# Low parts of five up units per turn made by an accumulating GpSimd DMA in the two gate/up stages

## The chip, the cores and the metric

The kernel runs on one core of one Trainium2 chip. The metric is device time of one execution in microseconds (us). The kernel before took 2433.75 us (median of 3 runs, 2433.02 to 2434.05).

## The reference

One decoder layer for 256 tokens of width 2048, in float32. The two feed-forward blocks are what the change touches; the width of each is 5632.

```
x = x + 0.5 * swiglu(rmsnorm(x, g_ffn1), w1_gate, w1_up, w1_down)
... (latent attention, dilated attention, gates, output projection)
x = x + 0.5 * swiglu(rmsnorm(x, g_ffn2), w2_gate, w2_up, w2_down)
... (per-layer embedding gate)
swiglu(h, wg, wu, wd) = (silu(h @ wg) * (h @ wu)) @ wd
```

All weights are float32 in HBM and are read once.

## The kernel before

Every product of float32 matrices is made of three matmuls of type float32r. A weight w is split into a rounded high part `wh` (the write to float32r rounds it) and a low part `wl` = w - `wh`; the activations are split alike. Then x w is taken as xh wh + xh wl + xl wh.

Weights stream in **units** of 128 x 1024 values (512 KB). Unit n uses slot n mod 4 of three rings, `raw`, `wh` and `wl`. Four engines work on it, each in its own fixed order, tied by counting semaphores:

- SP issues the load into `raw` (`square`, line 291) once the unit that used the slot before has its low part (`lo_ready`).
- ACT writes `wh` from `raw` (`split`, line 903, `hi_ready`) once the load has landed and PE is done with unit n-4 (`unit_done` at n-3).
- DVE writes `wl` = `raw` - `wh` (line 1310, `lo_ready`).
- PE waits for `lo_ready` and makes 12 matmuls of 512 columns (lines 444 to 446).

A gate/up stage has 11 **turns** of 512 output columns, with 16 units each, v0 to v15: even units are of the gate matrix, odd ones of the up matrix, and units 2p and 2p+1 are pair p, which covers two blocks of 128 rows. In turns 1 to 9 (`FAST_TURNS`) the pairs 1, 3 and 5 (`FAST_PAIRS`: v2, v3, v6, v7, v10, v11) are made by a scheme of Strassen's kind with 21 matmuls in place of 24 (lines 551 to 553). For it DVE also builds sums of weight blocks (`sums`, lines 1413 to 1416), ACT rounds them (`TH`, line 1000) and DVE takes their low parts (`TL`, line 1421). Before v14, PE turns the finished block of the turn before with 8 transposes (line 454). ACT and DVE work four units ahead: in the loop step of v they split v+4.

Both stages are written out unit by unit. The GpSimd engine (POOL) does nothing after the start.

Of the kernel before, what the change touches and what calls it, by code (L numbers as in the profile page):

```python
# [5 lines left out]
ALU = mybir.AluOpType  # L6
ACT = mybir.ActivationFunctionType
# [7 lines left out]
P = 128  # L15
BANK = 512
SLOTS = 4
# [32 lines left out]
def hybrid_layer(nc, out, x, p, positions, g_ffn1, w1_gate, w1_up, w1_down, g_mix, w_in, g_cq, w_uq,  # L50
# [16 lines left out]
    T, KD, KF = S // P, D // P, FF // P  # L67
# [7 lines left out]
    FFN_TURNS, FFN_BODY = FF // BANK, 2 * KD // 2  # L75
# [6 lines left out]
    UNITS = sum(counts)  # L82
# [3 lines left out]
    with ExitStack() as ctx:  # L86
        def sem(name):
            return ctx.enter_context(nc.semaphore(name))
# [27 lines left out]
        def whole(name, where, shape, dt=F32):  # L116
            return nc.alloc_sbuf_tensor_at(name, shape, dt, offset=front + where)
# [4 lines left out]
        raw = whole("raw", 48 * KB, [P, SLOTS, UNIT])  # L122
        wh = whole("wh", 64 * KB, [P, SLOTS, UNIT], F32R)
        wl = whole("wl", 80 * KB, [P, SLOTS, UNIT], F32R)
# [62 lines left out]
        raw_in = [sem(f"raw_in{j}") for j in range(SLOTS)]  # L187
        hi_ready, lo_ready = sem("hi_ready"), sem("lo_ready")
        unit_done = sem("unit_done")
        x_first, x_in = sem("x_first"), [sem(f"x_in{j}") for j in range(4)]  # L190
        ident_in, row1_in, rows_in, consts_in, gains_in, p_in = (
            sem(n) for n in ("ident_in", "row1_in", "rows_in", "consts_in", "gains_in", "p_in"))
# [38 lines left out]
        FAST_TURNS, FAST_PAIRS = range(1, FFN_TURNS - 1), (1, 3, 5)  # L231


        def fast(n):
            m, v = divmod(n, FFN_BODY)
            return n < FFN_TURNS * FFN_BODY and m in FAST_TURNS and v // 2 in FAST_PAIRS

        TURN_FASTS = len(FAST_TURNS) * len(FAST_PAIRS)
        FASTS = TURN_FASTS + 2 * len(DOWN_PAIRS)

# [8 lines left out]
        def fasts_down(r, half, k):  # L249

            return (r // 2) * FASTS + TURN_FASTS + half * len(DOWN_PAIRS) + DOWN_PAIRS.index(k // 2)

# [27 lines left out]
        def _(sp):  # L280
            def wide(n, j, w, k, c0, width=UNIT, waits=1):

                sp.wait_ge(lo_ready, n + waits - SLOTS)
                sp.dma_start(raw[:, j % SLOTS, 0:width], w[0, k * P:(k + 1) * P, ds(c0, width)])\
                  .then_inc(raw_in[j % SLOTS], 16)

            def square(n, j, w, k, c0, waits=1):

                if waits and not (isinstance(n, int) and n < SLOTS):
                    sp.wait_ge(lo_ready, n + waits - SLOTS)  # L290
                sp.dma_start(raw[:, j % SLOTS, :].rearrange("p (k c) -> p k c", k=2),
                             w[0, k * P:(k + 2) * P, ds(c0, BANK)].rearrange("(k p) c -> p k c", p=P))\
                  .then_inc(raw_in[j % SLOTS], 16)
# [53 lines left out]
            def projection(u0, c0):  # L347
                for k in range(KD):
                    wide(u0 + k, k, w_in, k, c0)
# [5 lines left out]
            for k in range(KD):  # L355
                wide(U_LAT + k, k, w_in, k, 0, LAT)
# [14 lines left out]
            j = 0  # L371
# [4 lines left out]
            with sp.Fori(1, MERGE_TURNS) as i:  # L376
                j = 0
                for w, c0, K in ((w_in, OFF_GATE, KD), (w_br_mla, 0, H), (w_in, OFF_GATE + D, KD), (w_br_dil, 0, H)):
                    for k in range(0, K, 2):


                        waits = 2 if j == KD // 2 - 1 else 0 if j == KD // 2 else 1
# [7 lines left out]
            j = 0  # L390
# [18 lines left out]
        def _(pool):  # L409
            for s in (a_ready, res_ready, dil_turned, dil_T, dil_ready, m_ready, mprod_ready):  # L410
                pool.sem_inc(s, PRIMED)
            pool.memset(ones[:, :], 1.0).then_inc(ones_ready, 1)


        @block.tensor
        def _(pe):
            def wide_tile(j, t, k, hi, lo, b0, width, K):

                s = j % SLOTS
                cols = [(c, min(width, c + BANK)) for c in range(0, width, BANK)]  # L420
                xh, xl = hi[:, k, t * P:(t + 1) * P], lo[:, k, t * P:(t + 1) * P]
                for a, w, first, last in ((xh, wh, k == 0, False), (xh, wl, False, False), (xl, wh, False, k == K - 1)):
                    for m, (c, e) in enumerate(cols):
                        mm = pe.matmul(ps[:, b0 + 2 * t + m, 0:e - c], a, w[:, s, c:e], start=first, stop=last)  # L424
                return mm

            def wide_unit(n, j, k, hi, lo, b0, width, K):

                pe.wait_ge(lo_ready, n + 1)
                for t in range(T):  # L430
                    mm = wide_tile(j, t, k, hi, lo, b0, width, K)
                mm.then_inc(unit_done, 1)

            def square_unit(n, j, k, hi, lo, b0, K):


                pe.wait_ge(lo_ready, n + 1)
                s = j % SLOTS
                for t in range(T):
                    for kk in range(2):  # L440
                        xh, xl = (a[:, k + kk, t * P:(t + 1) * P] for a in (hi, lo))
                        c = slice(kk * BANK, (kk + 1) * BANK)
                        first, last = k + kk == 0, k + kk == K - 1
                        pe.matmul(ps[:, b0 + t, :], xh, wh[:, s, c], start=first, stop=False)  # L444
                        pe.matmul(ps[:, b0 + t, :], xh, wl[:, s, c], start=False, stop=False)  # L445
                        mm = pe.matmul(ps[:, b0 + t, :], xl, wh[:, s, c], start=False, stop=last)  # L446
                mm.then_inc(unit_done, 1)
# [95 lines left out]
            def fast_pair(n, j, p, hi, lo, forms, sum_hi, sum_lo, first, last, b0, c12, c21, b1, count):  # L543

                s, s1, ka, kb = j % SLOTS, (j + 1) % SLOTS, 2 * p, 2 * p + 1

                def product(bank, x, w, start, stop):
                    (xh, xl), (yh, yl) = x, w  # L550
                    pe.matmul(ps[:, bank, :], xh, yh, start=start, stop=False)  # L551
                    pe.matmul(ps[:, bank, :], xh, yl, start=False, stop=False)  # L552
                    return pe.matmul(ps[:, bank, :], xl, yh, start=False, stop=stop)  # L553

                def block(k, t):
                    return hi[:, k, t * P:(t + 1) * P], lo[:, k, t * P:(t + 1) * P]

                def weights(slot, c):
                    return wh[:, slot, c * BANK:(c + 1) * BANK], wl[:, slot, c * BANK:(c + 1) * BANK]

                S1, S3, S2, S4 = forms
                T1, T3, T2, T4 = ((sum_hi[:, a, :], sum_lo[:, a, :]) for a in range(4))
                pe.wait_ge(lo_ready, n + 1)
                product(b0, block(kb, 0), weights(s, 1), False, False)
                product(b1, block(ka, 0), weights(s, 0), first, last).then_inc(unit_done, 1)
                pe.wait_ge(lo_ready, n + 2)
                product(c12, S4, weights(s1, 1), False, False).then_inc(unit_done, 1)
                pe.wait_ge(TL_ready, 2 * count + 1)
                product(b1 + 2, S3, T3, first, last)
                product(b1 + 3, S1, T1, first, last)  # L570
                pe.wait_ge(TL_ready, 2 * count + 2)
                product(b1 + 1, S2, T2, first, last)
                product(c21, block(kb, 1), T4, False, False).then_inc(fast_done, 1)
# [145 lines left out]
            for k in range(KD):  # L719
                if k == 10:  # L720
# [3 lines left out]
                    for a in range(2):  # L724
                        for h2 in range(H // 2):
                            for t in range(T):
                                c0 = (h2 % 2) * S + t * P
# [84 lines left out]
            j = KD  # L812
# [8 lines left out]
            with pe.Fori(1, MERGE_TURNS) as i:  # L821
                j = 0
# [26 lines left out]
            j = 0  # L849
            for h in range(2):  # L850
# [21 lines left out]
                if h == 0:  # L872
                    for k in range(PLE // P):
                        wide_unit(U_PLE + j, j, k, pTh, pTl, 4, UNIT, PLE // P)
                        j += 1
            pe.wait_ge(lo_ready, UNITS)
            for t, c0, c1, b in LAST:
                if b < 4:
                    pe.wait_ge(psig_ready, T + 1)
# [10 lines left out]
        def _(act):  # L890
# [5 lines left out]
            def split(n, j):  # L896

                first = isinstance(n, int) and n < SLOTS
                act.wait_ge(raw_in[j % SLOTS], ((n - j % SLOTS) * (16 // SLOTS) + 16) if not isinstance(n, int)
                            else 16 * (n // SLOTS + 1))  # L900
                if not first:
                    act.wait_ge(unit_done, n - (SLOTS - 1))
                act.activation(wh[:, j % SLOTS, :], raw[:, j % SLOTS, :], ACT.Copy).then_inc(hi_ready, 1)  # L903

            def ahead(n, j):
                split(n + SLOTS, j)
# [249 lines left out]
            for k in range(KD):  # L1156
# [10 lines left out]
                if k in (3, 4, 5, 6):  # L1167
                    if k == 3:
                        act.wait_ge(mla_inv, 1)
                    t, a = (k - 3) // 2, (k - 3) % 2  # L1170
                    for h in range(H):
                        c = (a * T + t) * H + h
                        src, step = ((q_tok, QK), (kv_tok, NOPE + HD))[a]
                        v = src[:, t, h * step:h * step + NOPE]
# [6 lines left out]
                if k in (11, 13):  # L1181
                    for h in range((k - 11) * 2, (k - 11) * 2 + 4, 2):
                        act.wait_ge(mla_turned, 2 + h + 1)
                        for a in range(2):
                            ins = act.activation(nT[:, h, a, :], ps[:, 4 + h % 4, a * S:(a + 1) * S], ACT.Copy,
                                                 scale=gcol[:, 4 * KD + NG + a:4 * KD + NG + a + 1])
# [77 lines left out]
            with act.Fori(0, MERGE_TURNS - 1) as i:  # L1264
                for j in range(MERGE_BODY):
                    n = U_MERGE + MERGE_BODY + i * MERGE_BODY + j
# [14 lines left out]
            j = 0  # L1281
# [22 lines left out]
        def _(dve):  # L1304
            chain = Chain(dve, dve_step)

            def split(n, j):

                dve.wait_ge(hi_ready, n + 1)
                dve.tensor_tensor(wl[:, j % SLOTS, :], raw[:, j % SLOTS, :], wh[:, j % SLOTS, :].bitcast(F32),  # L1310
                                  ALU.subtract).then_inc(lo_ready, 1)
# [362 lines left out]
            for k in range(KD):  # L1674
# [4 lines left out]
                if k < T:  # L1679
                    qr = rh[:, k, 0, :, :]  # L1680
                    q_rot = q_tok[:, k, :].rearrange("p (h c) -> p h c", h=H)[:, :, NOPE:QK]
                    c, s = (b[:, k, 0:half].unsqueeze(1).to_broadcast([P, H, half]) for b in (cos, sin))
# [119 lines left out]
            with dve.Fori(0, MERGE_TURNS - 1) as i:  # L1802
                for j in range(MERGE_BODY):
                    n = U_MERGE + MERGE_BODY + i * MERGE_BODY + j
# [14 lines left out]
            j = 0  # L1819
# [74 lines left out]
```

## Time and profile before

| | before |
|---|---|
| median of 3 runs | 2433.75 us |
| span of the profiled execution | 2432.5 us |
| PE busy, of the span | 2417.7 us, 99% |
| DVE busy | 1765.8 us, 73% |
| ACT busy | 1309.0 us, 54% |
| POOL busy | 0.4 us |
| DMA queue of SP | 455.52 MB, 58.8% of 16 engines |

The only times there are for the kernel as a whole are those of the three runs; the profiled execution has its span, from its first to its last instruction. A busy share is an average over stages. The first gate/up stage runs from the start to about 480 us, the second ends at about 2090 us. The timeline gives the start of an instruction, its length, and in brackets how long its engine sat idle before it and who ended that. A matmul is shown as 0.39 us long but the next starts 0.227 us later, since they overlap.

### The profile page before, as it was taken

The page shows a single profiled execution, that of the slowest core. Times are in us where ns is not written, and L with a number is a line of the kernel's source. Part 1 is how long each engine was busy: PE and PEld are TensorE (multiplying, and loading weights), DVE is VectorE, ACT ScalarE, POOL GpSimd, SP SyncE. Part 2 cuts the span into 40 slices and gives each one's busy share as a digit, 9 for nine tenths or more (in the row PEclk, how much of TensorE's full clock was granted, in tenths as well). Part 3 has the DMA queues.
Part 4 walks back from the last instruction along what each step waited for, and adds up shares of the span by engine and source line. Part 5 has one row for each costly group of instructions (what it writes and reads, how often), then busy time and mean ns, then how long its engine had stood idle before and what let it go on. Part 6 is the DMA issues. An engine that isn't in the chain of part 4 may idle for free.

```text
span 2432.5 us, 29257 instructions
## 1 busy us (share of the span) xinstructions
PE 2417.7 (99%) x11104; PEld 2009.4 (83%) x11104; DVE 1765.8 (73%) x2136; ACT 1309.0 (54%) x1594; POOL 0.4 (0%) x5
## 2 busy tenths in 40 slices
PE   9999999999999999999999999999999999999999
PEld 7888888878888877888888888888888888878887
DVE  6888989688876665657655455558898987787765
ACT  6555555554555665454454444455555555554553
POOL 0000000000000000000000000000000000000000
PEclk9999999999999999999999999999999999999999
DMA  7665656646656654655634666556565666566654
GB/s 241 195 212 182 214 184 207 199 166 214 191 188 193 182 157 132 196 182 181 191 116 127 200 190 191 189 184 201 184 207 183 205 200 201 180 200 200 206 186 165
DMA packets 192237, 457.54 MB, mean 188 GB/s; under 512 B 14632, under 2 KB 16624, under 8 KB 192112
## 3 DMA queue, kind: packets, MB, share of 16 engines
q1 hardware_dynamic: 191664, 455.52, 58.8%
q8 instruction: 80, 1.31, 0.2%
q14 instruction: 45, 0.37, 0.0%
q10 hardware_dynamic: 448, 0.34, 0.0%
HBM read 453.70 MB, written 2.10 MB: 187 GB/s over the span
## 4 chain that ended last, share of the span: by engine, by line
PE 95%; DVE 4%; ACT 1%; issue 0%; DMA 0%; SPq 0%; ACTq 0%
PE ps L424 37%; PE ps L444 13%; PE ps L446 13%; PE ps L445 13%; PE ps L551 5%; PE ps L553 5%; PE ps L552 5%; PE ps L622 1%; PE ps L454 1%; PE ps L638 1%; DVE wl L1310 1%; PE ps L462 1%; ACT wh L903 1%; PE ps L649 0%; DVE aTl L1471 0%
## 5 line engine op out<-in xcount | busy, mean ns | idle before, releaser
L1310 DVE TENSOR_TENSOR wl<-raw,wh 128x1024 fp32r<-128x1024 f32 x786 | 952.2, 1222 | 566.9 <-ACT wh L903 561.3
L903 ACT ACTIVATE wh<-raw 128x1024 fp32r<-128x1024 f32 x786 | 824.1, 1057 | 815.0 <-PE ps L424 400.1
L444 PE MATMUL ps<-wh,hT 128*128 128x512 f32 x1232 | 483.8, 393 | 2.1 <-DVE hT L1330 1.4
L446 PE MATMUL ps<-wh,hT 128*128 128x512 f32 x1232 | 480.1, 390 | 0.0
L445 PE MATMUL ps<-wl,hT 128*128 128x512 f32 x1232 | 480.0, 390 | 0.0
L424 PE MATMUL ps<-wh,hT 128*128 128x512 f32 (+1 forms) x1536 | 415.0, 388 | 1.2 <-DVE om L1576 1.0
L424 PEld LDWEIGHTS ps<-wh,hT 128*128 128x128 f32 x1536 | 283.6, 188 | 57.5 <-issue 1.2
L444 PEld LDWEIGHTS ps<-wh,hT 128*128 128x128 f32 x1232 | 231.8, 188 | 49.8 <-DVE hT L1330 1.7
L446 PEld LDWEIGHTS ps<-wh,hT 128*128 128x128 f32 x1232 | 231.6, 188 | 48.4
L445 PEld LDWEIGHTS ps<-wl,hT 128*128 128x128 f32 x1232 | 231.9, 188 | 46.7
L424 PE MATMUL ps<-wl,hT 128*128 128x512 f32 (+1 forms) x768 | 234.5, 387 | 0.0
L424 PEld LDWEIGHTS ps<-wl,hT 128*128 128x128 f32 x768 | 143.0, 188 | 29.1
L1000 ACT ACTIVATE TH<-sums 128x1024 fp32r<-128x1024 f32 x108 | 114.7, 1062 | 89.1 <-DVE sums L1413 65.9
L424 PE MATMUL ps<-wh,aTh 128*128 128x512 f32 x512 | 158.1, 390 | 0.0
L424 PE MATMUL ps<-wl,aTh 128*128 128x512 f32 x512 | 157.7, 389 | 0.0
L424 PE MATMUL ps<-wh,aTl 128*128 128x512 f32 x512 | 157.6, 389 | 0.0
L1421 DVE TENSOR_TENSOR TL<-sums,TH 128x1024 fp32r<-128x1024 f32 x108 | 127.1, 1218 | 0.0
L424 PEld LDWEIGHTS ps<-wl,aTh 128*128 128x128 f32 x512 | 96.1, 188 | 20.1
L424 PEld LDWEIGHTS ps<-wh,aTl 128*128 128x128 f32 x512 | 96.1, 188 | 20.0
L424 PEld LDWEIGHTS ps<-wh,aTh 128*128 128x128 f32 x512 | 95.7, 188 | 19.9 <-DVE wl L1310 0.2
L993 ACT ACTIVATE wh<-raw 128x512 fp32r<-128x512 f32 x78 | 49.3, 632 | 69.8 <-PE ps L446 30.4
L1000 ACT ACTIVATE TH_d<-sums_d 128x1024 fp32r<-128x1024 f32 x48 | 51.0, 1062 | 33.2 <-DVE sums_d L1413 22.3
(277 smaller groups left out, 2790.2 us busy)
## 6 DMA issues: line engine op xcount, KB each, us to landing
raw<-in_w_in SPq DMA_DIRECT2D x208, 512.0 KB, 3.6
raw<-in_w_gate SPq DMA_DIRECT2D x176, 512.0 KB, 3.7
raw<-in_w_up SPq DMA_DIRECT2D x176, 512.0 KB, 4.5
raw<-in_w_down SPq DMA_DIRECT2D x176, 512.0 KB, 4.4
raw<-in_w_o SPq DMA_DIRECT2D x32, 512.0 KB, 4.0
raw<-in_w_ple_gate SPq DMA_DIRECT2D x32, 512.0 KB, 3.5
raw<-in_w_br_mla SPq DMA_DIRECT2D x16, 512.0 KB, 4.8
raw<-in_w_br_dil SPq DMA_DIRECT2D x16, 512.0 KB, 3.7
```

Of the source, the lines that this page charges most:

```text
L424: mm = pe.matmul(ps[:, b0 + 2 * t + m, 0:e - c], a, w[:, s, c:e], start=first, stop=last)
L444: pe.matmul(ps[:, b0 + t, :], xh, wh[:, s, c], start=first, stop=False)
L445: pe.matmul(ps[:, b0 + t, :], xh, wl[:, s, c], start=False, stop=False)
L446: mm = pe.matmul(ps[:, b0 + t, :], xl, wh[:, s, c], start=False, stop=last)
L551: pe.matmul(ps[:, bank, :], xh, yh, start=start, stop=False)
L552: pe.matmul(ps[:, bank, :], xh, yl, start=False, stop=False)
L553: return pe.matmul(ps[:, bank, :], xl, yh, start=False, stop=stop)
L903: act.activation(wh[:, j % SLOTS, :], raw[:, j % SLOTS, :], ACT.Copy).then_inc(hi_ready, 1)
L993: act.activation(wh[:, s, BANK:UNIT], raw[:, s, BANK:UNIT], ACT.Copy).then_inc(hi_ready, 1)
L1000: act.activation(dst[:, 2 * a:2 * a + 2, :], src[:, 2 * a:2 * a + 2, :], ACT.Copy).then_inc(TH_ready, 1)
L1310: dve.tensor_tensor(wl[:, j % SLOTS, :], raw[:, j % SLOTS, :], wh[:, j % SLOTS, :].bitcast(F32), ALU.subtract).then_inc(lo_ready, 1)
L1421: dve.tensor_tensor(dst[:, 2 * a:2 * a + 2, :], src[:, 2 * a:2 * a + 2, :], hi[:, 2 * a:2 * a + 2, :].bitcast(F32), ALU.subtract).then_inc ...
```

## The change

Five units of each of the turns 1 to 9, v1, v5, v9, v13 and v15 (all of the up matrix, `by_dma`), get their low part in another way. ACT writes `wh` as before, then writes the negated rounded weight into `wl`, and only then counts up `hi_ready`. POOL waits for that and issues a DMA that reads the same 512 KB of weights from HBM once more and adds them to what stands in `wl`. DVE skips these units. PE waits for the DMA (`sum_in`) instead of `lo_ready`. SP frees the `raw` slot of such a unit by `hi_ready`. There are 45 such units in a stage and 90 in all. All counts of `lo_ready` are lowered by the number of such units before (`lows`).

```diff
+        def by_dma(n):
+            if not isinstance(n, int):
+                return False
+            n -= U_GU2 if n >= U_GU2 else U_GU1
+            m, v = divmod(n, FFN_BODY)
+            return m in FAST_TURNS and v % 2 == 1 and v // 2 not in FAST_PAIRS
...
@@ SP
                 if waits and not (isinstance(n, int) and n < SLOTS):
-                    sp.wait_ge(lo_ready, n + waits - SLOTS)
+                    if by_dma(n - SLOTS):
+                        sp.wait_ge(hi_ready, n - SLOTS + 1)
+                    else:
+                        sp.wait_ge(lo_ready, lows(n + waits - SLOTS))
...
@@ POOL
+            def low_parts(u0, w_gate, w_up):
+                for m in FAST_TURNS:
+                    for v in range(FFN_BODY):
+                        n, k, c0 = u0 + m * FFN_BODY + v, v // 2 * 2, m * BANK
+                        if by_dma(n):
+                            pool.wait_ge(hi_ready, n + 1)
+                            pool.dma_start(wl[:, n % SLOTS, :].rearrange("p (k c) -> p k c", k=2),
+                                           (w_gate, w_up)[v % 2][0, k * P:(k + 2) * P, c0:c0 + BANK]
+                                           .rearrange("(k p) c -> p k c", p=P), accum_op=ALU.add)\
+                                .then_inc(sum_in[n % SLOTS // 2], 16)
...
@@ PE, square_unit
-                pe.wait_ge(lo_ready, n + 1)
+                if by_dma(n):
+                    pe.wait_ge(sum_in[n % SLOTS // 2], 16 * sums_in(n))
+                else:
+                    pe.wait_ge(lo_ready, lows(n + 1))
...
@@ ACT, split
-                act.activation(wh[:, j % SLOTS, :], raw[:, j % SLOTS, :], ACT.Copy).then_inc(hi_ready, 1)
+                high = act.activation(wh[:, j % SLOTS, :], raw[:, j % SLOTS, :], ACT.Copy)
+                if by_dma(n):
+                    high = act.activation(wl[:, j % SLOTS, :], raw[:, j % SLOTS, :], ACT.Copy, scale=-1.0)
+                high.then_inc(hi_ready, 1)
...
@@ DVE, split
+                if by_dma(n):
+                    return
```

On ACT, before, from the split of v4 on in turn 2 (the last two rows make the sums of pair 3):

```order
L903 ACTIVATE wh<-raw 128x1024 [waits unit_done,raw_in0]
L903 ACTIVATE wh<-raw 128x1024 [waits unit_done,raw_in1]
L903 ACTIVATE wh<-raw 128x1024 [waits unit_done,raw_in2]
L993 ACTIVATE wh<-raw 128x512 [waits unit_done,raw_in3]
L1000 ACTIVATE TH<-sums 128x1024 [waits fast_done,sums_ready]
L1000 ACTIVATE TH<-sums 128x1024 [waits sums_ready]
```

The same place on ACT in the changed kernel:

```order
L941 ACTIVATE wh<-raw 128x1024 [waits unit_done,raw_in0]
L941 ACTIVATE wh<-raw 128x1024 [waits unit_done,raw_in1]
L943 ACTIVATE wl<-raw 128x1024
L941 ACTIVATE wh<-raw 128x1024 [waits unit_done,raw_in2]
L1034 ACTIVATE wh<-raw 128x512 [waits unit_done,raw_in3]
L1041 ACTIVATE TH<-sums 128x1024 [waits fast_done,sums_ready]
L1041 ACTIVATE TH<-sums 128x1024 [waits sums_ready]
```

One pass over the slot of v5 has come in between its high part and that of v6.

On SP, before, the loads of v4 to v9 of a turn:

```order
L291 DMA raw<-in_w_gate 128x2x512 [waits lo_ready]
L291 DMA raw<-in_w_up 128x2x512 [waits lo_ready]
L291 DMA raw<-in_w_gate 128x2x512 [waits lo_ready]
L291 DMA raw<-in_w_up 128x2x512 [waits lo_ready]
L291 DMA raw<-in_w_gate 128x2x512 [waits lo_ready]
L291 DMA raw<-in_w_up 128x2x512 [waits lo_ready]
```

The same loads in the changed kernel:

```order
L312 DMA raw<-in_w_gate 128x2x512 [waits lo_ready]
L312 DMA raw<-in_w_up 128x2x512 [waits hi_ready]
L312 DMA raw<-in_w_gate 128x2x512 [waits lo_ready]
L312 DMA raw<-in_w_up 128x2x512 [waits lo_ready]
L312 DMA raw<-in_w_gate 128x2x512 [waits lo_ready]
L312 DMA raw<-in_w_up 128x2x512 [waits hi_ready]
```

The order is the same; v5 and v9 now wait for ACT's second pass over v1 and v5 in place of DVE's low part.

On PE, before, the last rows of a unit and the start of v5, the fourth row here:

```order
L444 MATMUL ps<-wh,hT 128x512
L445 MATMUL ps<-wl,hT 128x512
L446 MATMUL ps<-wh,hT 128x512
L444 MATMUL ps<-wh,hT 128x512 [waits lo_ready]
L445 MATMUL ps<-wl,hT 128x512
L446 MATMUL ps<-wh,hT 128x512
```

The same place on PE in the changed kernel:

```order
L482 MATMUL ps<-wh,hT 128x512
L483 MATMUL ps<-wl,hT 128x512
L484 MATMUL ps<-wh,hT 128x512
L482 MATMUL ps<-wh,hT 128x512 [waits sum_in0]
L483 MATMUL ps<-wl,hT 128x512
L484 MATMUL ps<-wh,hT 128x512
```

Nothing moved; the wait ahead of the unit is now for the accumulating DMA. On POOL there are 90 DMAs `wl<-in_w_up`, each waiting for `hi_ready`, and nothing else.

## Rows read from the trace of the kernel before

**Rows 1.** Page, parts 1 and 2: busy us of each engine, and PE's granted clock.

```profile
PE 2417.7 (99%) x11104; PEld 2009.4 (83%) x11104; DVE 1765.8 (73%) x2136; ACT 1309.0 (54%) x1594; POOL 0.4 (0%) x5
...
PEclk9999999999999999999999999999999999999999
```

**Rows 2.** Windows (PE, PEld, DVE, ACT, POOL busy; clock; DMA share; GB/s): turn 2, both down stages.

```profile
100.33:142.70 42.37, 42.37 (x192) 35.18 (x192) 37.48 (x39) 24.14 (x26) 0.00 (x0) 1.00 0.63 199
483.00:700.00 217.00, 214.36 (x941) 176.51 (x940) 178.83 (x218) 116.84 (x127) 0.00 (x0) 0.99 0.59 195
2090.00:2300.00 210.00, 207.64 (x914) 171.55 (x913) 168.34 (x181) 113.19 (x120) 0.00 (x0) 0.99 0.58 192
```

**Rows 3.** Groups by line, 57 to 433 us: busy, mean ns, idle before.

```profile
L444 PE MATMUL ps<-wh,hT 128*128 128x512 f32 x353 | 138.0, 391 | 0.0
...
L903 ACT ACTIVATE wh<-raw 128x1024 fp32r<-128x1024 f32 x115 | 119.4, 1055 | 91.5 <-PE ps L446 48.7 <-DMA raw<-in_w_gate 40.2 <-DMA raw<-in_w_up 1.5
...
L1310 DVE TENSOR_TENSOR wl<-raw,wh 128x1024 fp32r<-128x1024 f32 x116 | 139.5, 1221 | 39.8 <-ACT wh L903 38.7
```

**Rows 4.** Waits of PE, 483 to 700 us: total, times, longest.

```profile
PE ps L551 <- DVE wl L1403: 2.5, 1, 2.5
```

**Rows 5.** Timeline of ACT, turn 2.

```profile
106.18 1.05 ACT L903 ACTIVATE wh<-raw 128x1024 fp32r<-128x1024 f32 x1
...
109.59 1.07 ACT L903 ACTIVATE wh<-raw 128x1024 fp32r<-128x1024 f32 x1 [2.36 <-DMA raw<-in_w_gate]
...
116.28 1.99 ACT L903 ACTIVATE wh<-raw 128x1024 fp32r<-128x1024 f32 x2
119.88 1.06 ACT L903 ACTIVATE wh<-raw 128x1024 fp32r<-128x1024 f32 x1 [1.61 <-DMA raw<-in_w_gate]
...
130.40 1.06 ACT L903 ACTIVATE wh<-raw 128x1024 fp32r<-128x1024 f32 x1 [0.21 <-DMA raw<-in_w_up]
131.37 0.58 ACT L969 ACTIVATE ends<-ps 128x512 f32<-128x512 f32 x1
...
136.68 1.06 ACT L903 ACTIVATE wh<-raw 128x1024 fp32r<-128x1024 f32 x1 [1.66 <-PE ps L446]
```

**Rows 6.** Timeline of PE, turn 2 and the start of turn 3.

```profile
105.82 0.39 PE L551 MATMUL ps<-wh,hT 128*128 128x512 f32 x1
...
113.30 0.39 PE L444 MATMUL ps<-wh,hT 128*128 128x512 f32 x1
...
116.02 0.39 PE L551 MATMUL ps<-wh,hT 128*128 128x512 f32 x1
...
123.50 0.39 PE L444 MATMUL ps<-wh,hT 128*128 128x512 f32 x1
...
133.70 0.39 PE L444 MATMUL ps<-wh,hT 128*128 128x512 f32 x1
...
136.42 1.03 PE L454 MATMUL ps<-ident,gs 128*128 128x128 f32 x8
...
140.03 0.39 PE L444 MATMUL ps<-wh,hT 128*128 128x512 f32 x1
...
145.47 0.39 PE L444 MATMUL ps<-wh,hT 128*128 128x512 f32 x1
```

**Rows 7.** DMA, 57 to 433 us: queue share; issues, KB, median us to landing.

```profile
q1 hardware_dynamic: 38848, 74.89, 62.0%
...
raw<-in_w_gate SPq DMA_DIRECT2D x74, 512.0 KB, 3.8
raw<-in_w_up SPq DMA_DIRECT2D x69, 512.0 KB, 4.6
```

**Rows 8.** Timeline of SP's DMA queue, turn 2: issue and its length.

```profile
105.71 0.37 SPq L291 DMA_DIRECT2D raw<-in_w_gate  x1
106.12 1.69 SPq L291 DMA_DIRECT2D raw<-in_w_up  x1
109.12 0.37 SPq L291 DMA_DIRECT2D raw<-in_w_gate  x1
111.58 0.37 SPq L291 DMA_DIRECT2D raw<-in_w_up  x1
```

More of the change, by code:

```diff
@@ L189, in hybrid_layer @@
         unit_done = sem("unit_done")
+        sum_in = [sem(f"sum_in{a}") for a in range(2)]
         x_first, x_in = sem("x_first"), [sem(f"x_in{j}") for j in range(4)]
@@ L236, in fast, with lows, sums_in @@
             return n < FFN_TURNS * FFN_BODY and m in FAST_TURNS and v // 2 in FAST_PAIRS
+        def by_dma(n):
[4 more added lines that the diff above has]
+            return m in FAST_TURNS and v % 2 == 1 and v // 2 not in FAST_PAIRS
+        def lows(n):
+            return n - (sum(by_dma(i) for i in range(n)) if isinstance(n, int) else TURN_DMAS)
+        def sums_in(n):
+            return sum(by_dma(i) and i % SLOTS == n % SLOTS for i in range(n + 1))
+        TURN_DMAS = len(FAST_TURNS) * (KD // 2 - len(FAST_PAIRS))
         TURN_FASTS = len(FAST_TURNS) * len(FAST_PAIRS)
@@ L289, in square @@
                 if waits and not (isinstance(n, int) and n < SLOTS):
-                    sp.wait_ge(lo_ready, n + waits - SLOTS)
+                    if by_dma(n - SLOTS):
+                        sp.wait_ge(hi_ready, n - SLOTS + 1)
+                    else:
+                        sp.wait_ge(lo_ready, lows(n + waits - SLOTS))
                 sp.dma_start(raw[:, j % SLOTS, :].rearrange("p (k c) -> p k c", k=2),
@@ L412, in _ @@
             pool.memset(ones[:, :], 1.0).then_inc(ones_ready, 1)
+            def low_parts(u0, w_gate, w_up):
[8 more added lines that the diff above has]
+                                .then_inc(sum_in[n % SLOTS // 2], 16)
+            low_parts(U_GU1, w1_gate, w1_up)
+            low_parts(U_GU2, w2_gate, w2_up)
         @block.tensor
@@ L434, in square_unit @@
             def square_unit(n, j, k, hi, lo, b0, K):
-                pe.wait_ge(lo_ready, n + 1)
+                if by_dma(n):
+                    pe.wait_ge(sum_in[n % SLOTS // 2], 16 * sums_in(n))
+                else:
+                    pe.wait_ge(lo_ready, lows(n + 1))
                 s = j % SLOTS
@@ L562, in fast_pair @@
                 T1, T3, T2, T4 = ((sum_hi[:, a, :], sum_lo[:, a, :]) for a in range(4))
-                pe.wait_ge(lo_ready, n + 1)
+                pe.wait_ge(lo_ready, lows(n + 1))
                 product(b0, block(kb, 0), weights(s, 1), False, False)
                 product(b1, block(ka, 0), weights(s, 0), first, last).then_inc(unit_done, 1)
-                pe.wait_ge(lo_ready, n + 2)
+                pe.wait_ge(lo_ready, lows(n + 2))
                 product(c12, S4, weights(s1, 1), False, False).then_inc(unit_done, 1)
@@ L875, in _ @@
                         j += 1
-            pe.wait_ge(lo_ready, UNITS)
+            pe.wait_ge(lo_ready, lows(UNITS))
             for t, c0, c1, b in LAST:
```

## The prediction

> **What bounds the kernel now.** I read the page's busy times first, then the windows of one turn and of the stages behind it, then the groups of instructions, and last the timelines of PE, ACT and SP over turn 2. PE is busy 2417.7 of 2432.5 us at a granted clock of nine tenths or more in each slice [rows 1]. In turn 2 it is busy for all of its 42.37 us, with the clock at 1.00, and its matmuls of 57 to 433 us had 0.0 us of idle time before them [rows 2, 3]. DVE is the second busiest there, 37.48 of 42.37 us, and ACT has 24.14 [rows 2]. So PE sets the time of these turns; work taken from DVE buys nothing while PE never waits for it. What decides is whether PE begins to wait.
>
> **What is removed.** 90 passes of DVE of 1.22 us [rows 3], 6.1 us a turn, 110 us in all. They lie beside PE, so I take their worth as 0. The one place where it could be more is behind the stage: PE waits 2.5 us for a low part in the first down stage and is idle 217.00 - 214.36 = 2.64 us there, and 210.00 - 207.64 = 2.36 us in the second [rows 2, 4]. Turn 10 keeps all its DVE work and stands in between, so that wait should stay. Bound: 0 to 5.0 us gained; I take 0.
>
> **What ACT gets.** 90 passes of some 1.06 us, the duration of its other passes of this size [rows 3], 5.3 us a turn: 24.14 + 5.3 = 29.4 of 42.37. Behind v5 ACT sat idle 2.36 us and behind v9 1.61 us until a load landed [rows 5], which hides the pass for all that follows. Behind v15 the copy of `ends` at 131.37 moves by one pass; PE needs what comes of it at 136.42 [rows 5, 6], and DVE has then two passes less in its queue. Cost of the pass itself to the others: 0. What it costs the unit is below, since the DMA starts behind it.
>
> **How long the DMA has.** PE must be done with unit n-4 before ACT writes, so the room for a low part is what is left of three units of PE time:
> - v5: ACT wrote its high part at 106.18 for 1.05 us. With the second pass `hi_ready` comes at 108.29, and PE starts v5 at 113.30 [rows 5, 6]. Room 5.0 us.
> - v9: v5 ends at 116.02, ACT starts 0.26 us behind an end of PE (136.68 against 136.42), and needs 2 x 1.06 us: 118.4. PE starts v9 at 123.50 [rows 5, 6]. Room 5.1 us.
> - v13: v9 ends 2.72 us after 123.50, so ready at 126.22 + 0.26 + 2.12 = 128.6, PE start 133.70 [rows 6]. Room 5.1 us.
> - v15: high part at 130.40, ready at 132.5, PE start 140.03 [rows 5, 6]. Room 7.5 us, and a stall at v13 widens it.
> - v1: high part at 136.68, ready at 138.8, PE start 145.47 [rows 5, 6]. Room 6.7 us.
>
> With a latency L from `hi_ready` to landing, a turn gets longer by 3L - 15.2, plus L - 6.7 if that is above zero. A stall does not repay itself: the next unit of the slot starts from PE's end of this one, so the same room opens again. There are 18 such turns.
>
> **What L is.** No DMA from POOL and no accumulating DMA is in the trace, so L has to be bounded. The nearest rows are plain loads of the same 512 KB issued by SP: 3.8 us for gate units and 4.6 us for up units, which mostly run behind a gate load [rows 7]. Floor: 3.8 us, as if the adding were free. For the top: a load keeps the 16 engines busy for 0.63 x 42.37 / 16 = 1.67 us [rows 2]. The adding has to read `wl` besides, which is a second stream, +1.67. And SP now sends its loads earlier, into the same time: v9's load went out at 111.58, when DVE had v5's low part, and now needs only `hi_ready` of v5 at 108.29; it leaves right behind v8's at 109.12 [rows 8]. Two loads beside it make +3.3. An issue took SP 0.37 us when the queue was free and 1.69 us when it was not [rows 8]; take 1.69 for POOL at most. Top: 3.8 + 1.67 + 3.3 + 1.69 = 10.5 us. I take 4.6 (one load ahead of it) + 1.67 (second read) + 1.2 (POOL's issue, nearer the upper of SP's two) = 7.5 us. By the floor a turn costs 0 and by the top 16.3 + 3.8 = 20.1 us.
>
> The row shows 1.67 us of the engines for one stream. The Trainium skill says in "Collectives: The Full Stack" (section "The bandwidth ceiling: the fold count and why AG ≠ RS ≠ AR") that adding costs no time by itself but needs two source reads on one ring, which halves the rate. By that rule the data part is twice a load's, as in my sum; if the read of `wl` were free L would be 5.8 us and the loss 40 us. No run here shows it yet.
>
> **Sum.** At L = 7.5 a turn gets 22.5 - 15.2 = 7.3, plus 0.8 for v1: 8.1 us. 18 turns: 146 us. The span goes from 2432.5 to 2578 us. The median of the runs lies 1.25 us above the span, so the time is 2580 us.
>
> **Rivals.**
> 1. *Hidden.* L is below 5.0 us and nothing changes: 2434 us. For it: both medians of the loads, 3.8 and 4.6 us, are below the room [rows 7]. Against it: these have no second read and no other issuing engine, and the contention grows. Chance 0.12.
> The Trainium skill gives in "DMA: Bandwidth & Descriptors", section "Anatomy of one DMA — SWDGE (gpsimd) path", 2.0 us plus bytes over 436 GB/s for a plain DMA from GpSimd, by estimate 3.2 us here. By it this rival would hold; the trace's own 3.8 to 4.6 us for plain loads is already longer.
> 2. *The DMA engines become the bound.* SP's 16 loads take 26.7 us of a turn (0.63 of 42.37) [rows 2]. Five adding DMAs at two loads' cost make 43.4 us of 42.37 + 8.1, which fits. From three loads' cost on (51.8 us) it does not, the queue grows, and raw loads are late too. At four the turn takes 16 + 20 = 36 times 1.67 = 60 us, 17.7 us more: 319 us, 2753 us. For it: the share is 0.63 already. Against it: the sum is exceeded only if the adding costs more than its two reads. Chance 0.2.
> 3. *Faster.* The lighter DVE enters turn 10 and the down stage with less behind it, and PE's wait of 2.5 us goes in both blocks, with the rest of the idle time: at most 5.0 us, 2429 us. It decides only if L stays below 5.0 us. Against it: turn 10 gives DVE time to catch up already. Chance 0.03.
>
> **How the numbers follow.** The main case, L between 5.1 and 9.5 us: 0.65. Its own range runs from 2435 us (L of 5.1) to 2434 + 18 x (13.3 + 2.8) = 2724 us (L of 9.5); its middle is the 2580. The range that should hold 8 in 10 takes in the hidden case and a part of the saturated one: 2432 to 2750. Some 0.02 lie below and 0.15 above. About 0.2% (4.9 us) is what a measurement can tell from no change. Faster by more: 0.02. Within it: the hidden case and the bottom of the main one, 0.13. Slower: 0.85.
>
> **What the profile of the changed kernel would show.** The window of one fast turn should be some 50 us long with PE busy for about 42. The list of waits should hold rows of PE waiting for the DMA of `wl` in three or four of 16 units, each some 2.4 us, the longest total of all PE rows. The issues should have 90 DMAs from POOL of 512 KB at about 7.5 us to landing. DVE should be near 31 of 50 us busy, ACT near 29, the DMA share about 0.85. ACT's high parts of v6, v10 and v14 should not have moved against PE. The stages outside turns 1 to 9 should keep their lengths. I am wrong if PE has no row of waiting for that DMA (hidden), if PE waits chiefly for `TL` or for ordinary `wl` (raw loads or ACT late, not the adding), if the granted clock falls in the stalls, or if the DMA share is near 1.

## The result, and the profile after

The changed kernel takes 2742.56 us (median of 4 runs, 2732.31 to 2745.54) against 2433.68 us before: a ratio of 1.1265, 95% interval 1.1251 to 1.1279. It is 309 us slower. The forecast was slower with 2580 us, a loss of 146 us: the sign and the place were right, the loss was half of what came.

The page of the changed kernel, its busy times, granted clock and the queues of SP (q1) and POOL (q0):

```profile
PE 2521.9 (92%) x11104; PEld 2063.5 (75%) x11104; DVE 1664.3 (61%) x2046; ACT 1388.4 (51%) x1684; POOL 108.9 (4%) x95
...
PEclk9999989899999999999999999998989989999999
...
q1 hardware_dynamic: 191664, 455.52, 53.1%
q0 software_dynamic: 24480, 47.19, 10.2%
```

Against [rows 1], PE's busy time grew by 104.2 us although it runs the same 11104 matmuls, and 220.1 us of the span are now without PE work, where 14.8 were. The two together are the 309.5 us by which the span grew (2742.0 us). DVE lost 101.5 us of work and ACT gained 79.4.

One turn, from one set of transposes to the next, in the columns of [rows 2]:

```profile
111.48:171.11 59.63, 47.05 (x189) 37.38 (x188) 31.91 (x33) 28.71 (x31) 6.01 (x5) 0.92 0.71 185
```

The turn that took 42.37 us takes 59.63, with PE at work for 47.05 of it and its clock at 0.92. DVE and ACT have time to spare, and the DMA share is 0.71, not near 1.

The waits of PE for the adding DMA (total, times, longest), the one row of PE above 5 us, where there was none before:

```profile
PE ps L482 <- DMA wl<-in_w_up: 205.4, 72, 5.0
```

72 waits are four in each of the 18 turns. In the timeline of PE over that turn they stand at v1, v5, v9 and v13:

```profile
121.94 0.50 PE L482 MATMUL ps<-wh,hT 128*128 128x512 f32 x1 [1.25 <-DMA wl<-in_w_up]
122.28 0.39 PE L483 MATMUL ps<-wl,hT 128*128 128x512 f32 x1
122.51 0.40 PE L484 MATMUL ps<-wh,hT 128*128 128x512 f32 x1
...
136.52 0.50 PE L482 MATMUL ps<-wh,hT 128*128 128x512 f32 x1 [4.08 <-DMA wl<-in_w_up]
...
151.80 0.79 PE L482 MATMUL ps<-wh,hT 128*128 128x512 f32 x1 [3.18 <-DMA wl<-in_w_up]
152.40 0.63 PE L483 MATMUL ps<-wl,hT 128*128 128x512 f32 x1
152.82 0.63 PE L484 MATMUL ps<-wh,hT 128*128 128x512 f32 x1
...
167.71 0.50 PE L482 MATMUL ps<-wh,hT 128*128 128x512 f32 x1 [4.07 <-DMA wl<-in_w_up]
```

Behind the short wait of 1.25 us the matmuls start 0.23 us apart from the second on, as before. Behind the one of 3.18 us they start 0.42 us apart: this is the lower of the two clock levels, 1.2 in place of 2.4 GHz. Behind the one of 4.08 us the first few still start 0.23 us apart, and from 137.55 us on 0.39 to 0.43. That is where PE's additional busy time comes from. By the mean granted clock the loss is (1 - 0.962) x 2742.0 = 104 us, and 5 us before (0.998); this is an estimate from above, since the mean also counts time at the lower level in which PE stood still. Here is the clock of the changed kernel:

```profile
core 0: 2742.0 us, clock 0.962
```

How v5 of this turn comes about, in the timelines of ACT, POOL and SP:

```profile
125.06 1.06 ACT L941 ACTIVATE wh<-raw 128x1024 fp32r<-128x1024 f32 x1 [1.35 <-PE ps L484]
126.02 1.04 ACT L943 ACTIVATE wl<-raw 128x1024 fp32r<-128x1024 f32 x1
127.75 1.06 ACT L941 ACTIVATE wh<-raw 128x1024 fp32r<-128x1024 f32 x1 [0.68 <-DMA raw<-in_w_gate]
```

```profile
127.36 1.20 POOL L441 DMA_DIRECT2D wl<-in_w_up  x1 [12.11 <-ACT wl L943]
```

```profile
126.55 0.37 SPq L312 DMA_DIRECT2D raw<-in_w_gate  x1
127.09 0.37 SPq L312 DMA_DIRECT2D raw<-in_w_up  x1
```

ACT is ready at 127.06 us, POOL begins 0.30 us later and is at work until 128.56, and PE goes on at 136.52, 9.5 us after ACT. The loads of v8 and v9 went out at 126.55 and 127.09 and run beside the adding DMA. Compare [rows 8]: before, 2.5 us lay between these two loads. The issues of the changed kernel, with the median us to landing, and all landings of POOL's DMAs:

```profile
raw<-in_w_gate SPq DMA_DIRECT2D x176, 512.0 KB, 4.4
raw<-in_w_up SPq DMA_DIRECT2D x176, 512.0 KB, 4.6
...
wl<-in_w_up POOLq DMA_DIRECT2D x90, 512.0 KB, 8.3
```

```profile
L441 POOL DMA_DIRECT2D wl<-in_w_up x90: 1203/1203/1332, 53.2 to 2338.5; - x90
...
DMA to landing us min/median/max: 6.5/8.3/10.8
```

### The profile page after: what moved, and what is told of

Its sections match the earlier page's. It is cut to its first block, busy times and chain, and to the rows that moved or that the text cites. A ratio compares the mean times of both kernels' runs of the same rounds, so it can differ in the third digit from the quotient of the medians.

```text
span 2742.0 us, 29347 instructions
## 1 busy us (share of the span) xinstructions
PE 2521.9 (92%) x11104; PEld 2063.5 (75%) x11104; DVE 1664.3 (61%) x2046; ACT 1388.4 (51%) x1684; POOL 108.9 (4%) x95
## 3 DMA queue, kind: packets, MB, share of 16 engines
q0 software_dynamic: 24480, 47.19, 10.2%
## 4 chain that ended last, share of the span: by engine, by line
PE 68%; DMA 22%; ACT 6%; DVE 3%; issue 2%; ACTq 0%; SPq 0%
PE ps L459 34%; DMA wl<-in_w_up 22%; PE ps L482 10%; PE ps L484 9%; PE ps L483 9%; ACT wh L941 3%; ACT wl L943 3%; PE ps L589 1%; PE ps L591 1%; PE ps L590 1%; PE ps L660 1%; PE ps L676 1%; DVE wl L1353 1%; PE ps L500 1%; PE ps L687 0%
## 5 line engine op out<-in xcount | busy, mean ns | idle before, releaser
L1353 DVE TENSOR_TENSOR wl<-raw,wh 128x1024 fp32r<-128x1024 f32 x696 | 847.0, 1223 | 959.6 <-ACT wh L941 956.0
L482 PE MATMUL ps<-wh,hT 128*128 128x512 f32 x1232 | 526.0, 427 | 207.3 <-DMA wl<-in_w_up 205.4
L483 PE MATMUL ps<-wl,hT 128*128 128x512 f32 x1232 | 511.7, 415 | 0.0
L484 PE MATMUL ps<-wh,hT 128*128 128x512 f32 x1232 | 511.2, 415 | 0.0
L482 PEld LDWEIGHTS ps<-wh,hT 128*128 128x128 f32 x1232 | 249.6, 203 | 289.0 <-DMA wl<-in_w_up 235.7
L459 PEld LDWEIGHTS ps<-wh,hT 128*128 128x128 f32 x1536 | 283.6, 188 | 57.4 <-issue 1.2
L484 PEld LDWEIGHTS ps<-wh,hT 128*128 128x128 f32 x1232 | 250.5, 203 | 56.8
L483 PEld LDWEIGHTS ps<-wl,hT 128*128 128x128 f32 x1232 | 251.4, 204 | 50.7
L441 POOL DMA_DIRECT2D wl<-in_w_up x90 | 108.5, 1205 | 2229.8 <-ACT wl L943 2216.4
L459 PEld LDWEIGHTS ps<-wl,hT 128*128 128x128 f32 x768 | 143.0, 188 | 29.1
L943 ACT ACTIVATE wl<-raw 128x1024 fp32r<-128x1024 f32 x90 | 93.9, 1043 | 0.0
```

The source lines that it names most:

```text
L441: pool.dma_start(wl[:, n % SLOTS, :].rearrange("p (k c) -> p k c", k=2), (w_gate, w_up)[v % 2][0, k * P:(k + 2) * P, c0:c0 + BANK] .rearra ...
L943: high = act.activation(wl[:, j % SLOTS, :], raw[:, j % SLOTS, :], ACT.Copy, scale=-1.0)
```

## The experiments

Each was timed in three rounds beside the kernel before. Edits are against the changed kernel. Times are medians; waits, clock and latency are those of the profiled run, and the latency is the median from issue to landing. In 2 and 11 the profiled run is not the typical one: its clock is 0.996 and 0.994, those of the other three runs are 0.993 to 0.994 and 0.996 to 0.997.

| kernel | us | ratio, 95% interval | PE waits for the DMA, us (times) | clock | DMA to landing, us |
|---|---|---|---|---|---|
| changed | 2742.56 | 1.1251 to 1.1279 | 205.4 (72) | 0.962 | 8.3 |
| 1 second pass only | 2432.84 | 0.999 to 1.001 | 0 | 0.999 | |
| 2 copy, nothing added | 2502.8 | 1.0274 to 1.0309 | 47.4 (34) | 0.996 | 6.1 |
| 3 stalls filled | 2664.24 | 1.0931 to 1.0967 | 20.5 (31) | 0.998 | 8.2 |
| 4 only v15 | 2443.6 | 1.0028 to 1.0061 | 6.6 (8) | 0.998 | 8.6 |
| 5 only v5 | 2534.72 | 1.0394 to 1.0428 | 67.4 (18) | 0.985 | 8.2 |
| 6 loads later | 2602.33 | 1.0675 to 1.0711 | 117.3 (71) | 0.987 | 6.1 |
| 7 negated first | 2591.73 | 1.0634 to 1.0669 | 115.8 (67) | 0.987 | 7.8 |
| 8 relief only | 2431.87 | 0.9986 to 1.0006 | 0 | 0.999 | |
| 9 half filled | 2674.14 | 1.097 to 1.1017 | 105.0 (71) | 0.993 | 8.3 |
| 10 = 6 and 7 | 2547.79 | 1.0461 to 1.0496 | 77.4 (60) | 0.991 | 6.2 |
| 11 = 2 and 6 | 2482.86 | 1.0187 to 1.0221 | 32.8 (28) | 0.994 | 4.6 |

**1. The second pass alone.** No unit goes to the DMA; ACT still makes the pass for the same 90 units (`neg_too` names them), and DVE then writes over it.

```diff
-            return m in FAST_TURNS and v % 2 == 1 and v // 2 not in FAST_PAIRS
+            return False
...
-            return n - (sum(by_dma(i) for i in range(n)) if isinstance(n, int) else TURN_DMAS)
+            return n
...
-                if by_dma(n):
+                if neg_too(n):
                     high = act.activation(wl[:, j % SLOTS, :], raw[:, j % SLOTS, :], ACT.Copy, scale=-1.0)
```

> ACT makes its second pass over the 90 units, but DVE then makes all low parts as before and there is no DMA from POOL. Theory (the loss is the wait for the adding DMA and what follows from it): the pass hides, 2434 us, within 0.2%. Rival (a fuller ACT delays high parts or sums and PE waits for them): some 1 us for each pass, 18 x 5 x 1.04 = 94 us, 2528 us.

It cost nothing that can be measured. ACT's busy time rose to 1391.5 us as it should.

**8. The relief alone.** DVE skips the units and nothing replaces its work.

```diff
-            low_parts(U_GU1, w1_gate, w1_up)
-            low_parts(U_GU2, w2_gate, w2_up)
...
-                    pe.wait_ge(sum_in[n % SLOTS // 2], 16 * sums_in(n))
+                    pe.wait_ge(hi_ready, n + 1)
```

> ACT makes its second pass and DVE skips the 90 units, but no DMA is issued and PE takes wl as it is (negated high parts in place of low parts, so that part of the computation is left out). It shows what the lighter DVE is worth by itself. Theory (PE is the bound and DVE's work is hidden): 2434 us, at most the 5 us of idle time behind the stages less, 2429. Rival (DVE's load is on the path at places that PE's idle times don't show): 2420 us or less.

101 us less of DVE work (1664.1 us busy against 1765.8) are worth 3.4 us at most by the interval, 0.9986 to 1.0006, and may be worth nothing. So the change had next to nothing to win even if the DMA were free.

**2. Copying in place of adding.** The kernel leaves out the addition, so its low parts are wrong.

```diff
-                                           .rearrange("(k p) c -> p k c", p=P), accum_op=ALU.add)\
+                                           .rearrange("(k p) c -> p k c", p=P))\
```

> The 90 DMAs from POOL only copy the weights into wl, nothing is added (the low parts are then not right and the output is not the reference's). Theory A (the adding costs a second stream): the latency of 8.3 us falls by some 2 us to 6.3, a turn stalls 3 x 1.2 = 3.7 us, 67 us in all, and with the clock lost behind 54 gaps (1.7 us each, 92 us) up to 2593 us. Rival B (the latency is POOL's way of issuing and contention, adding is free): 8.3 us as before, 2743 us.

The latency went as theory A said: it fell from 8.3 to 6.1 us. The queue and issue rows of this kernel:

```profile
PE 2438.5 (98%) x11104; PEld 2012.6 (81%) x11104; DVE 1664.7 (67%) x2046; ACT 1389.0 (56%) x1684; POOL 64.8 (3%) x95
...
q0 software_dynamic: 24480, 47.19, 6.1%
...
wl<-in_w_up POOLq DMA_DIRECT2D x90, 512.0 KB, 6.1
```

For the same 47.19 MB the queue's packets took 0.061 x 2499.0 = 152 us of the 16 engines against 0.102 x 2742.0 = 280 us: 1.7 us for one copy and 3.1 us for one addition, a factor of 1.8. POOL's instruction is shorter as well, 64.8 / 90 = 0.72 us against 1.20. The clock hardly fell, so the up to 92 us that I gave it were wrong here: the waits were 1.4 us on average.

**11. Copying, with the next load behind it** (the edits of 2 and 6).

> The DMAs from POOL only copy (nothing is added, so the low parts are not right), and SP sends the next load of the slot behind them. It completes the table of latencies: adding beside the loads 8.3 us, copying beside them 6.1, adding with the load behind 6.1. Theory (adding costs some 2.2 us through its second stream, the load beside it another 2.2 us, and they are separate): 4 to 4.7 us to landing, under the room of 5.0, so no stall from the DMA itself; the chain landing, load 4.1, two passes 2.1, copy 4.3 is 10.5 us against 10.2, so 2440 to 2465 us. Rival (both only stand for one contention, which either removes): the latency stays at about 6 us, 2500 us or more.

The latency is as forecast, 4.6 us; the time is not, 2483 us, above the forecast of 2440 to 2465. The loads now come late: ACT waits 95.9 us for those of the up matrix, PE still waits 32.8 us for the DMA, and the clock costs 15 us (0.994) in this run. The four latencies are 8.3 (adding, load beside), 6.1 (copying, load beside), 6.1 (adding, load later) and 4.6 us (copying, load later). By these medians adding costs 1.5 to 2.2 us and the load beside it as much again. It is a rough split: "later" holds back one load, and others still overlap the DMA, and by unit the latencies differ. With the load beside, copies took 4.2 us for v5 and 7.3 for v15, additions 7.9 for v1 and 10.3 for v15 (medians of 18).

**6. The load behind the adding DMA.**

```diff
                     if by_dma(n - SLOTS):
-                        sp.wait_ge(hi_ready, n - SLOTS + 1)
+                        sp.wait_ge(sum_in[n % SLOTS // 2], 16 * sums_in(n - SLOTS))
```

> SP sends the load that follows in the slot of a DMA unit only when the adding DMA has landed, in place of at ACT's second pass, so this load no longer runs beside it. Theory A (contention with the loads is a part of the latency): it falls from 8.3 to 7.5 us or less, stalls fall by 2.5 us a turn, 2690 us or less. Rival B (the latency is the DMA's own: POOL's 1.2 us, two streams, landing): the latency stays, and the later loads cost something: 2743 us or more, up to 2800.

Theory A, and stronger than forecast: the latency fell to 6.1 us and the kernel is 140 us faster by one wait of SP. The price shows in ACT's waits of this kernel; on SP's loads of the up matrix it waited 172.4 us:

```profile
ACT wh L941 <- DMA raw<-in_w_up: 172.4, 55, 6.2
PEld ps L482 <- DMA wl<-in_w_up: 147.3, 71, 4.2
PE ps L482 <- DMA wl<-in_w_up: 117.3, 71, 3.8
```

The chain through the slot now goes over the late load: 4.1 us to its landing, two passes, 6.1 us.

**7. The negated pass first.** ACT writes `wl` before `wh`, and POOL waits for the first of the two. PE waits for both.

```diff
+                if by_dma(n):
+                    act.activation(wl[:, j % SLOTS, :], raw[:, j % SLOTS, :], ACT.Copy, scale=-1.0).then_inc(neg_ready, 1)
                 high = act.activation(wh[:, j % SLOTS, :], raw[:, j % SLOTS, :], ACT.Copy)
...
-                            pool.wait_ge(hi_ready, n + 1)
+                            pool.wait_ge(neg_ready, n + 1 - lows(n))
...
                 if by_dma(n):
+                    pe.wait_ge(hi_ready, n + 1)
                     pe.wait_ge(sum_in[n % SLOTS // 2], 16 * sums_in(n))
```

> ACT makes the negated pass first and POOL waits for it alone, so the adding DMA is issued one pass (1.04 us) earlier while ACT writes the high part. Theory (the stall is latency less room): each of the four stalls of a turn gets 1.04 us shorter (v1's by what it has): 128 us of stalls in place of 205, and the clock still drops behind most gaps (2.2 us each), 2640 to 2665 us. Rival (the stall is set by something else than this chain, such as the DMA engines' share): 2743 us as before.

The stalls are as forecast: 115.8 us in the rows and, with 0.16 us more for each of the 67 (see experiment 3), 127 against 128 us. The clock loss is smaller than I gave it, 0.987 being 34 us in place of 104, so the time lies below the forecast of 2640 to 2665 us. The latency fell as well, from 8.3 to 7.8 us, so not all of the gain is the earlier issue. The edit took 151 us off the kernel: PE stood still for 89 us less and was busy for 60 us less (2461.4 us against 2521.9), the clock's part.

**10. Both 6 and 7.**

> Both: the negated pass first (2592 us alone) and the load behind the adding DMA (2602 us alone). The chain of a slot is then landing of the sum, load 4.1 us, negated pass 1.04 us, adding DMA 6.1 us: 11.2 us against four units of PE, 10.2 us. Theory (these two are separate terms of one chain): stalls of 1 to 1.3 us at v5, v9 and v13, 54 to 70 us in all, no clock loss: 2490 to 2510 us. Rival (both only uncover the same next wait, the late raw load): no better than the better of the two, 2590 us.

The time lies between the two theories. It beats the better of the two kernels by 44 us and misses the forecast by 38. ACT still waits 148.3 us for up loads, PE 77.4 us for the DMA, and the clock costs 23 us (0.991), which I had left out.

**3. The stalls filled.** Ahead of the wait PE multiplies by a matrix of zeros into a bank that is being accumulated.

```diff
                 if by_dma(n):
+                    v = (n - (U_GU2 if n >= U_GU2 else U_GU1)) % FFN_BODY
+                    pe.wait_ge(zeros_ready, 1)
+                    for _ in range({1: 5, 15: 0}.get(v, 14)):
+                        pe.matmul(ps[:, b0 - 2, :], zeros[:, :], hT[:, 0, :, :].rearrange("p a s -> p (a s)"),
+                                  start=False, stop=False)
                     pe.wait_ge(sum_in[n % SLOTS // 2], 16 * sums_in(n))
```

> Ahead of the wait for the adding DMA, PE makes matmuls of a zero matrix into a bank that is being accumulated (14 of 512 columns for v5, v9 and v13, 5 for v1), about as long as the stall they stand in. Theory A (of the 309 us lost, 205 are stalls and 104 are matmuls at 0.43 us in place of 0.227 because the granted clock drops behind each gap): the stalls are filled, the clock stays at 1.00 and the time falls to 2434 + 205 = 2639 us, 2635 to 2660. Rival B (the slow matmuls come from something else that goes on at that time, such as the DMA's traffic): the clock and the time stay, 2743 us or a little more.

The 846 zero matmuls at 0.227 us are 192 us of work, and the kernel is 78 us faster with them, 4 us above the forecast of at most 2660. The window of the same 59.63 us as above:

```profile
111.48:171.11 59.63, 58.41 (x259) 47.48 (x259) 35.53 (x37) 30.90 (x34) 6.01 (x5) 1.00 0.77 199
```

The clock is 1.00 where it was 0.92, with the same DMAs beside it at the same latency (8.2 us): rival B, that something else that goes on at that time, such as the DMA's traffic, slows PE, falls. Zero matmuls (192), waits left (20.5) and the clock (0.4 more than before) make 213 of the 231 us. A wait costs up to 0.16 us more than its row says, since a matmul is shown 0.39 us long; for 72 places that is 12 us. Some 7 us stay open.

**9. Half filled**, with 7 and 2 zero matmuls in place of 14 and 5.

> As the filled kernel, but with 7 zero matmuls ahead of v5, v9 and v13 and 2 ahead of v1, about half the stall. The other half, some 1.6 us, stays a gap. Theory (the clock drops behind the long gaps, not behind ones like the 47.4 / 34 = 1.4 us of the kernel that adds nothing): the clock stays near 1.00 and less PE work is added than with 14: 2434 + 205 = 2639 us, up to 2650, below the 2664 of the filled one. Rival (any gap in this place drops the clock, only a full one keeps it): 2434 + 205 + 90 = 2730 us.

A miss. The clock did stay near 1 (0.993, 14 us more than before), but the time is 2674 and not 2639 to 2650. Zero matmuls (414 x 0.227 = 94 us), waits (105 + 11 for their hidden part) and clock (14) make 224 of 241 us; 17 us stay open. Part is visible as a slower start behind a wait: above, the first two starts behind the wait of 1.25 us are 0.34 us apart. At 0.11 us more for each of 71 waits that is 8 us at most. Half a filling is no better than a full one.

**4 and 5. One unit of a turn alone**, here v15; for v5 the same with `(5,)`.

```diff
-            return m in FAST_TURNS and v % 2 == 1 and v // 2 not in FAST_PAIRS
+            return m in FAST_TURNS and v in (15,)
...
-        TURN_DMAS = len(FAST_TURNS) * (KD // 2 - len(FAST_PAIRS))
+        TURN_DMAS = len(FAST_TURNS) * 1
```

> Only v15 of each turn is made by the DMA (18 in all), the unit with the most room: 7.5 us, and with no stall before it at v13. At a latency of 8.3 us it would stall PE 0.8 us a turn, 14 us, 2448 us, more if the clock drops behind so short a gap (up to 2480). With 16 loads and one adding DMA a turn the latency should be shorter, 7 to 7.5 us, and then nothing changes: 2434 us. The lighter DVE (1.2 us a turn) is worth nothing by either. Rival (DVE's load did matter): below 2429 us.

> Only v5 of each turn is made by the DMA (18 in all), room 5.0 us. Theory (the room is what three units of PE leave, and the latency is the DMA's own, 8.3 to 8.6 us): stalls of 3.3 to 3.6 us, 59 to 65 us, and the clock lost behind each gap, 1.7 us x 18 = 31 us: 2524 to 2530 us. Rival (the latency comes from five such DMAs a turn standing in each other's way, alone it is near 6 us): 18 to 25 us of stalls, no clock loss, about 2455 us.

v15 alone: 2443.6 us, 10 us more, since the latency did not shorten (8.6 us). It is near the first of my two figures, 2448. PE waited in 8 of 18 turns only: the room of 7.5 us was read in one turn, and over the turns of this kernel it was 7.6 to 9.3 us. v5 alone: 101 us more, 2534.7 against a forecast of 2524 to 2530. Its 18 waits sum to 67.4 us, and the clock of 0.985 costs 38 us less the 5 of before. So a single adding DMA per turn, with nothing of its kind beside it, takes as long (8.2 us) as each of five, and the rival that they stand in each other's way falls.

## Why the prediction was right or wrong

- **What bounds the kernel:** right. PE was the bound, and the lighter DVE was worth nothing that can be measured (experiment 8). The time outside turns 1 to 9 kept its length to 2 us in all.
- **ACT's pass at 0:** right (experiment 1). Its price was the later DMA, and 7 shows how much that weighs.
- **The room:** right. Over the 18 turns of the changed kernel its medians were 5.2 us for v5, v9 and v13 and 6.8 for v1, where I had 5.0, 5.1, 5.1 and 6.7. v15 never had to wait, as forecast. With L = 8.3 us my sum gives 3 x 8.3 - 15.2 + 8.3 - 6.7 = 11.3 us a turn, 203 us in all. That PE's waits were 205.4 is partly luck. I counted L from `hi_ready`, and 8.3 us counts from the issue, 0.30 us later; the rows of waits leave out 0.16 us each, so that PE stood 217 us in all. From ACT's second pass to PE's start it took 8.2 us for v1 and v9, 8.5 for v5 and 9.3 for v13 (medians).
- **The latency L:** mis-sized, and nearer than it deserved. I put 7.5 us and it was 8.3. POOL's instruction took 1.20 us, just the 1.2 that I chose, and the second stream's share was right in kind. What I put in the top of the range only, and left out of the value, was the load that SP now sends beside the DMA. Experiment 6 prices it at 2.2 us. Without it the latency is 6.1, so what I did count was 1.4 us too much, and the two errors cancel but for 0.8. This term was 146 us and should have been 217.
- **The clock:** the step that failed. The sum had no such term; I only wrote that a falling clock would prove me wrong. Of the 309 us, some 93 are slower matmuls, nearly all at the lower level (104.2 us of busy time less 72 x 0.16 us of matmul tails), and 205.4 + 12 are stalls. So the forecast of 146 us lacked 93 us of clock and 71 of stalls. Counted in the timelines, the clock fell behind 48 of the 72 waits; the median of these waits was 3.3 us, and of the others 1.4 us. In 18 of the 48 a few matmuls still ran at the upper level first. [rows 1] said nothing of it because PE hardly ever stood still. But the trace of before did hold it, behind the very waits for DVE that I had read for the down stages. The one of 2.5 us in [rows 4] ends at 536.43 us, and from 538.48 us on matmuls stand 0.43 us apart; in the second down stage they do so at once:

```profile
2142.58 0.79 PE L551 MATMUL ps<-wh,aTh 128*128 128x512 f32 x1 [2.36 <-DVE wl L1403]
2143.17 0.63 PE L552 MATMUL ps<-wl,aTh 128*128 128x512 f32 x1
2143.59 0.63 PE L553 MATMUL ps<-wh,aTl 128*128 128x512 f32 x1
```

  The Trainium skill has this in "TensorE: Matmul & The Clock Gate", section "HAM oscillation — how this bites in real kernels": a wait for a DMA between groups of matmuls lets the clock fall, so that each group starts slow. This case agrees, 0.962 of the clock with the stalls and 0.998 with them filled, though not behind every wait, and the rule would have been a rival.
- **Rival 2**, the DMA engines as the bound, named 2753 us, close to what came, by a mechanism that was not there: the DMA share was 0.71 in the turn, and one adding DMA per turn had the latency of five. The main case ended at 2724 us, so that the measured time lies below the 2750 of my range is owed to this rival alone.
- **The two rules that the prediction took from the Trainium skill.** The one of two source reads in "Collectives: The Full Stack" (section "The bandwidth ceiling: the fold count and why AG ≠ RS ≠ AR") held: the addition took 1.8 times the engine time of a copy (2 against the changed kernel) and 1.7 times (11 against 6: 0.072 x 2488.6 and 0.117 x 2599.5 us of the 16 engines). The one of 2.0 us plus bytes over 436 GB/s in "DMA: Bandwidth & Descriptors" (section "Anatomy of one DMA — SWDGE (gpsimd) path") did not, in a kernel in which other loads run: even the copy with the next load held back took 4.6 us (experiment 11), not 3.2.
- **The check list:** DVE and ACT as said (31.9 and 28.7 us in the turn), waits in four of 16 units. PE did not wait for `TL` or for an ordinary `wl` in the turns. The wait was 2.85 us each and not 2.4, the turn 59.6 us and not 50, the DMA share 0.71 and not 0.85.

## What to carry to other kernels

Work that is taken from an engine that no one waits for is worth nothing, and its replacement must fit into the time that the ring of slots leaves. That time can be read from the trace of before, here to 0.2 us for the four units that PE then waited for, but in several turns: v15's differed from turn to turn by almost 2 us. What is missing is paid again each time that the slot comes round. Where PE would begin to stall, add the clock to the sum: here each microsecond of stall cost almost another half, and filling the stalls with idle matmuls won 78 us of it back. When a change frees a buffer earlier, ask which load goes out earlier and what it runs beside: to hold that load back took 2.2 us off the latency here and 140 us off the kernel.

## What the runs showed of the hardware

- A 512 KB DMA from POOL that adds in SBUF lands after 8.3 us beside the next load of its slot and 6.1 us with that load held back; one that copies after 6.1 and 4.6 us. These are medians of 90, with other loads still about. SP's loads of the gate and up matrices in the kernels of the table that issue such DMAs have medians of 3.8 to 4.8 us.
- Its instruction on POOL takes 1.20 us, 0.72 us for a copy. It is nearly the same for all 90: 1203 to 1222 ns for the 71 that overlap a `tensor_tensor` of DVE, and up to 1332 ns for the others. The Trainium skill infers this in "SBUF — State Buffer" (Who interferes with whom): a `tensor_tensor` of DVE takes only the shared read interface and writing descriptors needs the other. The trace agrees, with DVE busy for 31.91 of 59.63 us in the turn.
- The length of the wait alone does not say whether the clock falls: in the changed kernel it fell behind one of 1.8 us and not behind one of 3.1. In kernel 5, with one wait a turn of 2.6 to 5.1 us, it fell behind 17 of 18, and the one without a fall was of 3.3 us. What decides stays open.
